# Second tile's output projection in four parts of four matmuls, its residual and the later queries one group later

## The reference, cut to what matters

```python
h = h + merged @ w_out[l]
h = h + peer(rmsnorm(h, g_ffn[l]), ...)

def peer(x, wq, keys, u_tab, v_tab):
    q = (x @ wq).reshape(B, L, PEER_HEADS, 2, D_HALF)       # 8 heads
    s = einsum('blhpd,hpkd->blhpk', q, keys)
    ts, ti = top_k(s, 16)
    cand = ts[..., 0, :, None] + ts[..., 1, None, :]
    cs, ci = top_k(cand.reshape(B, L, PEER_HEADS, 256), 16)
    experts = ...                                           # one of 16384, per token, head and pick
    g = softmax(cs)
    act = gelu(einsum('td,tkd->tk', xt, u_tab[et])) * gt
    return einsum('tk,tkd->td', act, v_tab[et])
```

## Time and profile before

| | |
|---|---|
| median of 3 runs | 2089.93 us (2085.76 to 2095.61) |
| the profiled execution, its own time | 2090.83 us |
| its span in the trace | 2089.1 us |
| TensorE busy | 1768.7 us, 85% of the span |
| VectorE busy | 771.6 us, 37% |
| GpSimd busy | 299.1 us, 14% |
| DMA over the span | 761.80 MB, mean 365 GB/s |

### The profile page before, as it was taken

How to read it: one execution, slowest core, us unless ns; L and a number is a source line. 1 busy time by engine, 2 the same in 40 slices (tenths; PEclk the granted TensorE clock), 3 DMA queues, 4 the chain that set the end, 5 groups by cost and what they waited for, 6 DMA issues and landing times. The chain is left out here.

```text
span 2089.1 us, 23422 instructions
## 1 busy us (share of the span) xinstructions
PE 1768.7 (85%) x9328; PEld 914.3 (44%) x9328; DVE 771.6 (37%) x1877; ACT 423.4 (20%) x990; POOL 299.1 (14%) x284
## 2 busy tenths in 40 slices
PE   9999986886766555668999999888799999998886
PEld 7779862553321111124554444233377544442332
DVE  3955176776667777854230000000213300000002
ACT  2481122221222112223121010000123201110001
POOL 0000033453334444440000000000000000000000
PEclk9999998998886876689999999999999999999999
DMA  7236279999999999997789999999944999999996
GB/s 262 93 131 290 101 299 388 409 415 422 422 421 421 421 421 421 421 420 302 292 360 428 426 428 427 426 426 426 423 181 187 412 427 426 427 427 427 427 426 277
DMA packets 78973, 761.80 MB, mean 365 GB/s; under 512 B 8628, under 2 KB 9621, under 8 KB 17542
## 3 DMA queue, kind: packets, MB, share of 16 engines
q1 hardware_dynamic: 41190, 489.34, 56.1%
q0 software_dynamic: 37664, 270.84, 31.5%
HBM read 759.10 MB, written 1.05 MB: 364 GB/s over the span
## 5 line engine op out<-in xcount | busy, mean ns | idle before, releaser
L2584 PE MATMUL bank<-arena 128*64 128x512 f32 x3072 | 684.3, 599 | 55.3 <-DMA arena<-in_w_up 19.6
L1057 PE MATMUL bank<-arena 64*64 64x512 f32 x2032 | 324.6, 794 | 233.7 <-ACT arena L772 233.6
L2584 PEld LDWEIGHTS bank<-arena 128*64 128x64 f32 x3072 | 233.8, 138 | 492.0 <-issue 470.8
L563 POOL DMA_INDIRECT arena<-in_peer_uv,arena x256 | 287.4, 1123 | 631.5 <-PE bank L1057 305.9
L1401 DVE CUSTOM_DVE_ANT_0 arena<-arena 128x1024 f32<-128x1024 f32 x256 | 313.6, 1225 | 171.2 <-DMA arena<-in_peer_uv,arena 168.0
L1057 PEld LDWEIGHTS bank<-arena 64*64 64x64 f32 x2032 | 93.9, 177 | 444.8 <-ACT arena L772 265.7
L2711 DVE TENSOR_TENSOR arena<-arena,bank 128x512 f32<-128x512 f32 x32 | 22.0, 687 | 718.5 <-PE bank L2584 718.5
L822 PE MATMUL bank<-arena 128*128 128x272 f32 (+2 forms) x768 | 145.2, 349 | 0.5 <-ACT arena L596 0.3
L822 PEld LDWEIGHTS bank<-arena 128*128 128x128 f32 x768 | 126.4, 191 | 19.9 <-issue 2.5
L767 ACT ACTIVATE arena<-arena 128x4 f32<-128x4 f32 (+1 forms) x65 | 13.3, 205 | 466.4 <-DVE arena L1401 466.4
L1487 POOL DMA_DIRECT2D arena<-in_w_router x2 | 1.1, 574 | 562.4 <-POOLq L2469 528.0
(11 more groups left out here) (444 smaller groups left out, 1482.9 us busy)
## 6 DMA issues: line engine op xcount, KB each, us to landing
arena<-in_w_up SPq DMA_DIRECT2D x64, 2048.0 KB, 36.9
arena<-in_w_gate SPq DMA_DIRECT2D x64, 2048.0 KB, 32.9
arena<-in_w_down SPq DMA_DIRECT2D x64, 2048.0 KB, 39.0
arena<-in_w_in SPq DMA_DIRECT2D x13, 2048.0 KB, 8.5
arena<-in_w_out SPq DMA_DIRECT2D x2, 4096.0 KB, 17.9
arena<-in_wq SPq DMA_DIRECT2D x4, 2048.0 KB, 13.6
arena<-in_rg_out SPq DMA_DIRECT2D x1, 4096.0 KB, 13.9
arena<-in_peer_uv,arena POOLq DMA_INDIRECT x256, 17.4
```

What stands on the lines that cost most here:

```text
L563: nc.gpsimd.indirect_dma_start(SLOT[slot_of[j]], None, d["peer_uv"], bass.IndirectOffsetOnAxis(IDX[:, u % 4, k:k + 1], 0)).then_inc(s_row[ ...
L1057: m = pe.matmul(bank[banks[t][half]][to:to + HALF, :], DIAG[lo:lo + HALF, k + j, :], row[lo:lo + HALF, D + half * 512:D + (half + 1) * 512 ...
L2584: x = pe.matmul(bank[b][j * C:(j + 1) * C, :], operand[:, c, j * C:(j + 1) * C], RING[s % AHEAD][:, c % (DC // 2), j, :], start=(c == 0), ...
```

## The change

`w_out` takes a `part`, the range of the eight matmuls that it issues; it signals only with the last of the eight. The two calls of eight behind groups 1 and 2 become four of four, behind groups 1, 2, 3 and 4. `turn(1)`, ScalarE's `root(1)` and `turned(1)`, and VectorE's `residual(1)` each move one group later. Queries g = 4 to 15, and with them their scores and the copies out of PSUM, also move one group later, to groups 6 to 17.

```diff
--- before.py
+++ after.py
@@ -390,7 +390,7 @@
     QUERIES = ((0, 0, 0, 2, 4, 5), (0, 0, 2, 4, 6, 7)) + tuple(
         (t, k, lo, lo + 2, 4, 5) for t, k in ((0, 1), (0, 2), (1, 0), (1, 1), (0, 3), (1, 2), (1, 3)) for lo in (0, 2))
     NQ = len(QUERIES)
-    QUERIES_AFTER = {0: 3, **{g + 1: g for g in range(4, NQ)}}
+    QUERIES_AFTER = {0: 3, **{g + 2: g for g in range(4, NQ)}}
     LAST_WITH = [1 + max(g for g in range(NQ) if QUERIES[g][1] == k) for k in range(4)]
     SCORES_AFTER = {n + 1: g for n, g in QUERIES_AFTER.items()}
     MEMORY = [(layer, kind, i) for layer in range(2) for kind in range(2) for i in range(2)]
@@ -780,9 +780,9 @@
                         exps(1)
                     if n == 3:
                         exps(2)
-                    if n == 4:
+                    if n == 5:
                         root(1)
-                    if n == 6:
+                    if n == 7:
                         turned(1)
                     if u and q == 2 and u + 2 < UNITS:
                         exps(u + 2)
@@ -951,12 +951,13 @@
                     if o % 4 == 3:
                         m.then_inc(s_rom, 1)
 
-            def w_out(t, n):
+            def w_out(t, n, part=range(DC)):
                 te.wait_ge(s_mg, 2 * t + 2)
-                for c in range(DC):
+                for c in part:
                     m = pe.matmul(bank[WO_BANKS[t][n]][:, :], G2[:, c, t * P:(t + 1) * P],
                                   WOUT[:, c, n * 512:(n + 1) * 512], start=(c == 0), stop=(c == DC - 1))
-                m.then_inc(s_wm, 1)
+                if part[-1] == DC - 1:
+                    m.then_inc(s_wm, 1)
 
             def turn(t):
                 te.wait_ge(s_xf, t + 1)
@@ -1061,9 +1062,9 @@
                             if half:
                                 m.then_inc(s_pv, 1)
                     if k % Q == Q - 2:
-                        if n in (1, 2):
-                            w_out(1, n - 1)
-                        if n == 5:
+                        if n in (1, 2, 3, 4):
+                            w_out(1, (n - 1) // 2, range((n - 1) % 2 * 4, (n - 1) % 2 * 4 + 4))
+                        if n == 6:
                             te.wait_ge(s_res, 4)
                             turn(1)
                         if n in SCORES_AFTER:
```

## The result

The changed kernel takes 2103.42 us (median of 7 runs, 2101.05 to 2107.29) against 2089.93 us before (7 runs, 2085.76 to 2095.61). The ratio is 1.0053, with a 95% interval of 1.0042 to 1.0065: slower by 0.5%, at the very edge of what I had called no change. The profiled execution took 2103.19 us, 12.4 more than before. The median stands 1.4 us above the upper end of my range. The ratio is not that of the two medians (1.0065, the upper end of the interval); applied to 2089.93 it gives 2101.0, which is inside by 1.0 us. Both stand above my own range of 2095.5 to 2099.6, before I widened it by 3 us for the spread of the runs.

The account below looks back on a forecast made before the run. The gather stage was taken to be bound by DMA transfers, 2.48 us per pick. Cost 8.4 less gain 1.8 gave +6.6 us: 2097.4 us for the profiled execution, forecast median 2096.5, range 2089 to 2102.

Parts of the forecast that it names:

- the gate: Wait of pick 50's gather for queries g = 9, with only picks 48 and 49 queued; forecast cost 8.4 us.
- Part 4: Queries one group later: pick 50 issued at 422.0 instead of 413.80, landing at 428.7 instead of 422.1; cost 8.4 us.
- Part 1: w_out in four parts: group 2 begins 2.9 us earlier; 2.8 us gained, 1.0 lost at pick 20, net 1.8.
- Part 3: Residual, root and turn one group later: the same delay falls one group later; zero, between -0.4 and +0.6 us.
- Part 2: Query weights issued at about 339.4 instead of 323.75, same bytes: moving them costs nothing.
- rival B: TensorE meets group 11 at the lower clock, pick 50 issued 1.7 us later: 2101.3, slower by over 0.5%; chance 0.13.
- Rival A: Hole at pick 50 given back over picks 52 to 255, only the gain stays: faster, 2088.1; chance 0.07.
- C: Query weights land late, TensorE stands until 376.5, 6.8 us more: 2103.3, slower by over 0.5%; chance 0.05.
- D: Gain and cost meet, query weights or loads filling part of the hole: no visible change, 2088 to 2092; chance 0.10.

Follow-up runs that it names:

- e11: Kernel before with only the first half of each of the two later query weight tiles loaded, 2 MB less: ratio 0.9970.
- e2: Kernel before with only queries g = 4 to 15 moved one group later; w_out, residual and turn stay: ratio 1.0047.
- e1: Changed kernel with the new slots (8 to 11) first used at pick 52 instead of 48: ratio 1.0000.
- e4: Kernel before with queries g = 4 to 15 one group later and the new slots first used at pick 52 instead of 48: ratio 0.9999.
- e7: Kernel before with the two calls of w_out(1, .) cut to four matmuls each at their old places: ratio 1.0001.
- e12: Kernel before with the second of the two later query weight tiles issued only when queries g = 4 are done: ratio 1.0003.
- e5: Changed kernel with dummy matmuls in TensorE's idle time behind groups 0 to 5, 7, 9 and 11: ratio 1.0053.
- e6: Changed kernel with dummy matmuls behind groups 0 to 5, 7, 9 and 11, and new slots first used at pick 52: ratio 1.0010.
- e8: Kernel before with dummy matmuls behind groups 0, 3, 4, 6, 8, 10 and 11: ratio 1.0010.
- e10: Kernel before with fewer dummy matmuls, behind groups 0, 3, 4, 6, 8 and 11: ratio 1.0004.
- e9: Changed kernel with new slots first used at pick 52 and about half the dummy matmuls of e6: ratio 1.0012.

## Why the prediction was right or wrong

- **What the range owes to luck.** I forecast +6.6 us and the ratio gives +11.1 (8.8 to 13.6). The direction and the place of the loss were right, the size was short by 4.5 us: up to 1.4 us of it in the gate's cost (8.4 forecast, 8.6 to 9.8 measured) and 1.8 us in a gain that no run shows; the rest is inside the interval. The result lies in the range only because I had added 3 us for the spread of the runs.
- **What bounds the stage: right as far as seen.** 2 MB less made the kernel 6.3 us faster (e11, 4.9 us of it at pick 31 in the trace), and the 8.6 us lost at the gate stand at the end. Not all that is won early stays won, as e11's own trace shows.
- **Part 4, the gate: right, in place and size.** The cost was forecast at 8.4 us; it was 8.6 in the changed kernel's trace, 9.8 us for this part alone in the timed runs (e2), and nothing when six picks are queued (e1, e4). The issue itself came 14.0 us later and not 8.2, because group 11 began late (419.64), 2.47 us behind pick 47, which was itself late. The same lateness explains why pick 50 came only 11.4 us behind pick 47 + 2 x 2.48, where I had named 12 to 15. Pick 50's own dot product began 5.7 us behind its issue on the empty queue, where I had 6.7, and pick 51's 3.65 us behind that, where I had 2.48: together 9.3 us against 9.2. The estimate of 4.4 us from the Trainium skill (DMA: Bandwidth & Descriptors, anatomy of one GpSimd DMA) is again below what the trace shows for pick 50, 5.7 us.
- **Part 1, the gain from four parts: not borne out.** The step in doubt is the sum "2.8 - 1.0 = 1.8 us, net gain". Its first half held: group 2 early, the stretch at 316 full. Of a gain at the end no run shows anything: e1 and e4, which differ by this part, are equal within about 2.5 us. I took a closed hole for time won. e7 closes the same hole and ends at 1.0001, and its trace shows what I had left out: the chain on VectorE. Routing, residual(1) and the dot products of two groups fill 342.9 to 361.0 there, so picks that land earlier are not used earlier and the next gathers go out no sooner. In the changed kernel it was another way: from pick 15 to pick 31, the stretch that this part reaches, its trace gained 1.9 us (51.6 us instead of 53.5), and lost 1.65 before it and 3.2 behind it. The 1.9 us are no proof either: e2, without the split, took 50.8 us for the same picks. The losses fall at groups 1, 6 and 8, whose first gather went out 3.96 to 4.05 us behind the group's start instead of 2.96, 2.71 and 2.22. That these losses come from the change is not shown.
- **Part 3, residual: right here, but not as a rule.** I hid its 5.1 us under transfers. In the changed kernel that is so (picks 26 and 27 wait for transfers, 5.52 and 1.25 us). In e7 it is part of the chain on VectorE that decides.
- **Part 2, query weights: moving them costs nothing that the runs can see** (e12, 1.0003, one tile later; e1, 1.0000, both later), but they fill a hole at a price: the gathers that share the queue with them come late (e7).
- **Half clock (rival B): in the trace at groups 1, 3, 5, 6, 8 and 10, not at group 11,** where rival B put its price, so B is out as it stands. At group 6 it took 4.05 us from the group's start to the first issue (365.63 to 369.68), against 2.72 at group 2. Filling TensorE's idle time won nothing back in the timed runs.
- **Rival A (given back): out**, the late slices are at 420 to 422. **C (weights late): out**, queries g = 4 began right behind turn(1) at 371.5. **D (gain and cost meet): out**, the changed kernel is 8.8 to 13.6 us slower.
- **How much of the extra 4.5 us before pick 47 is the change?** Changed kernel and e1 are the same up to there and differ by 3.4 us (138.7 and 135.3); e2 and e4 likewise (134.3 and 137.7). 1.5 us of it stand already at pick 11, where no instruction has changed. So of the 4.5 us in one pair of traces the greater part can be such spread. The timed runs bound it: about 11 us in all (0.53% of 2090), of which e1 takes away all, within 2.3 us.

Open: what would win back the early losses (from pick 11 to pick 47 before: 105.5 us, of which 36 x 2.48 = 89.3 are picks and 10.0 the query weights, so 6.2 us lost; 9.2 in the changed kernel's trace). Neither less work on TensorE (e7), nor dummy matmuls in its idle time (e5, e6, e8 to e10), nor the weights elsewhere (e12) did.

## What to carry to other kernels

A table that says "one step later" can move a release that another engine's in-order queue waits for: look up what each counted semaphore gates, and count what that queue holds in reserve at that moment; here two gathers (5 us of transfer) stood against a wait of 17.9 us, and moving the gate by four picks took the whole cost away. In a loop of several engines with two sets of buffers a closed hole is only won time if the next turn of the loop starts earlier too; read the next issue, not the stretch that has filled up. When two profiles of identical instructions can differ by 3 us, judge such steps by timed variants, and say how little these can tell too: with 12 runs each, here, a step under 2.5 us stays open.

## What the runs showed of the hardware

The idle time before a group did not by itself decide its clock, as I had read it. Two groups met by TensorE after nearly the same idle time, the first in e6 and the second in e9 (which also has a group 6 at half clock after 8.11 us):

```profile
398.10 5.30 PE L1059 MATMUL bank<-arena 64*64 64x512 f32 x32 [2.05 <-ACT arena L773]
```

```profile
365.73 5.25 PE L1059 MATMUL bank<-arena 64*64 64x512 f32 x32 [8.11 <-ACT arena L773]
...
397.60 3.66 PE L1059 MATMUL bank<-arena 64*64 64x512 f32 x32 [2.07 <-ACT arena L773]
```

After 2.05 us it took 5.30 us, after 2.07 us it took 3.66. So what I wrote of rival B, that it decides from an idle time between 2.08 and 3.44 us, does not hold: 2.05 us was already followed by a slow group. The same instructions also meet other groups at half clock in another execution: group 1 took 6.46 us in the changed kernel and 3.66 in e1, whose instructions up to there are the same. That may be a source of the spread up to pick 47; no run here tested it by itself.
